# One transformer program on one core: work moved across the edges between its stages

## The reference

```python
def second_block(x, p, norm_g, ...):
    for i in range(DEPTH_2):                      # 2 layers
        g = norm_g[i]
        x = x + FFN_RESIDUAL * rmsnorm_2(swiglu(rmsnorm_2(x, g[0]), ffn_w_in[i, 0], ffn_w_out[i, 0]), g[1])
        h = rmsnorm_2(x, g[2])
        ...                                       # m: diff_attention (i = 0) or s5_glu (i = 1)
        x = x + rmsnorm_2(m, g[3])
        x = x + FFN_RESIDUAL * rmsnorm_2(swiglu(rmsnorm_2(x, g[4]), ffn_w_in[i, 1], ffn_w_out[i, 1]), g[5])
        gate = jax.nn.sigmoid(rmsnorm_2(x, g[6]) @ ple_w_gate[i])
        x = x + rmsnorm_2(gate * (p[i] @ ple_w_proj[i]), g[7])
    return x

def swiglu(h, w_in, w_out):                       # D_FF = 2816
    gu = h @ w_in
    return (jax.nn.silu(gu[..., :D_FF]) * gu[..., D_FF:]) @ w_out
```

## Time and profile before

| | us |
|---|---|
| median of 3 runs | 2223.03 (2222.31 to 2223.61) |
| the profiled execution, its own time | 2225.54 |
| its span, first to last instruction | 2223.8 |
| PE busy | 1993.2 (90%) |
| DVE busy | 1387.0 (62%) |
| ACT busy | 1079.7 (49%) |
| the chain that ended last | PE 65%, DVE 24%, ACT 7%, issue 3%, DMA 1% |
| mean granted TensorE clock | 0.933 |
| a feed-forward unit's transfer, issue to landing (median) | 6.3 |

### The profile page before, as it was taken

The page is one execution under the profiler, slowest core; times in us unless marked ns, Lnnn a source line. Parts: engine busy times, 40 slices in busy tenths (PEclk is TensorE's granted clock), DMA queues, the critical chain, the costliest instruction groups (busy, mean ns, idle before and its releaser), DMA issues.

```text
span 2223.8 us, 29527 instructions
## 1 busy us (share of the span) xinstructions
PE 1993.2 (90%) x11984; PEld 1737.5 (78%) x11984; DVE 1387.0 (62%) x1905; ACT 1079.7 (49%) x1563; POOL 0.2 (0%) x4
## 2 busy tenths in 40 slices
PE   7996899999999978998998899878997599889987
PEld 5885666666666658997887899768997477789976
DVE  4635899999999965564334555435564995255542
ACT  3333788888888864443234434334443221343431
POOL 0000000000000000000000000000000000000000
PEclk9997999999999999998999999999999576999998
DMA  6325888989989864542343454234542000445420
GB/s 243 112 73 199 311 333 330 342 328 341 338 338 336 335 239 154 188 165 73 124 135 149 146 195 167 105 113 156 186 166 91 38 1 23 177 146 195 167 76 19
DMA packets 45661, 408.71 MB, mean 184 GB/s; under 512 B 4800, under 2 KB 10432, under 8 KB 11344
## 3 DMA queue, kind: packets, MB, share of 16 engines
q1 hardware_dynamic: 40688, 398.86, 48.8%
q10 hardware_dynamic: 4832, 7.90, 1.1%
HBM read 405.66 MB, written 1.08 MB: 183 GB/s over the span
## 4 chain that ended last, share of the span: by engine, by line
PE 65%; DVE 24%; ACT 7%; issue 3%; DMA 1%; ACTq 0%; DVEq 0%; SPq 0%
PE wk L1474 23%; DVE ws_moe L1007 12%; PE acc L1455 11%; PE wk L353 7%; ACT ws_moe L1000 3%; PE wk L913 3%; PE wk L1730 3%; PE wk L359 2%; DVE sq L1074 2%; PE wk L959 2%; PE wk L311 2%; DVE rstd L283 2%; PE acc L705 1%; ACT hT L321 1%; PE acc L1759 1%
## 5 line engine op out<-in xcount | busy, mean ns | idle before, releaser
L1007 DVE TENSOR_TENSOR ws_moe<-ring,ws_moe 128x1024 fp32r<-128x1024 f32 x384 | 452.0, 1216 | 41.9 <-ACT ws_moe L1000 41.0
L1000 ACT ACTIVATE ws_moe<-ring 128x1024 fp32r<-128x1024 f32 x384 | 392.0, 1051 | 83.3 <-PE wk L913 72.3
L1474 PE MATMUL wk<-hx,gu_ffn 128*128 128x256 f32 x2112 | 269.0, 288 | 26.6 <-DVE gu_ffn L1404 26.6
L1474 PEld LDWEIGHTS wk<-hx,gu_ffn 128*128 128x128 f32 x2112 | 264.7, 198 | 27.3 <-issue 27.3
L1474 PE MATMUL wk<-hx,gu 128*128 128x256 f32 x2112 | 277.3, 290 | 4.5 <-DVE hx L1491 4.5
L1474 PEld LDWEIGHTS wk<-hx,gu 128*128 128x128 f32 x2112 | 266.1, 195 | 9.1 <-DVE hx L1491 6.7
L959 PE MATMUL wk<-ws_moe,xp_moe 128*128 128x512 f32 x1024 | 271.7, 408 | 1.5 <-issue 1.5
L1455 PE MATMUL acc<-hh_ffn,dn_ffn 128*128 128x256 f32 x2112 | 267.1, 283 | 0.0
L1455 PEld LDWEIGHTS acc<-hh_ffn,dn_ffn 128*128 128x128 f32 x2112 | 259.5, 192 | 0.0
L1434 ACT ACTIVATE hT<-hT 128x256 f32<-128x256 f32 x88 | 36.9, 419 | 392.3 <-DVE hT L1506 392.3
L959 PEld LDWEIGHTS wk<-ws_moe,xp_moe 128*128 128x128 f32 x1024 | 189.6, 190 | 45.1 <-issue 2.4
(11 more groups left out here) (331 smaller groups left out, 2497.3 us busy)
## 6 DMA issues: line engine op xcount, KB each, us to landing
ring<-in_u_moe SPq DMA_DIRECT2D x129, 1536.0 KB, 8.3
ring<-in_u_ffn SPq DMA_DIRECT2D x88, 1536.0 KB, 6.3
ring<-in_u_qkv SPq DMA_DIRECT2D x12, 1024.0 KB, 4.9
ring<-in_u_ple SPq DMA_DIRECT2D x8, 1280.0 KB, 5.4
ring<-in_u_in SPq DMA_DIRECT2D x9, 1024.0 KB, 4.9
ring<-in_u_glu SPq DMA_DIRECT2D x8, 1024.0 KB, 5.0
ring<-in_u_out SPq DMA_DIRECT2D x4, 1024.0 KB, 4.8
ring<-in_u_o SPq DMA_DIRECT2D x4, 1024.0 KB, 5.0
```

The source lines that it names most:

```text
L1000: e.activation(WS[:, n % NWS, 0, :], piece(x), ACT.Copy).then_inc(s.m_hi, 1)
L1007: e.tensor_tensor(WS[:, n % NWS, 1, :], piece(x), WS[:, n % NWS, 0, :].bitcast(F32), SUB).then_inc(s.m_lo, 1)
L1474: m = e.matmul(b[:, a * T:(a + 1) * T], gu_of(c, f)[:, x, a * 1024 + k * 128:a * 1024 + (k + 1) * 128], HX[:, y, k, :], start=k == 0 and a ...
```

## The change

Six things are done:

- In a feed-forward part, the split of unit 1's gate and up weights and of unit 0's down weights stands ahead of the root on ScalarE and ahead of the reciprocal on VectorE. An activation of one column (`tiny`) with Silu stands behind the root.
- A stage's last additions (`add_act`): an activation of one column with Sqrt stands ahead of the copies, and the root stands behind the sixth copy instead of the eighth.
- A feed-forward part's last down products signal after every second tile (`f_end`), and each pair of squares waits for its own.
- The experts' last products signal after every second tile (`m_last`), and VectorE adds in four pairs. ScalarE no longer waits for the fence before unit 0's split, and reads x in part 0 pair by pair. What is still in use at the end of the experts was moved to a second scratch tensor (`scrb`) behind the others, so that unit 0's split may be written early.
- In an embedding all four projections stand ahead of the sums.
- `pT` is fetched in the feed-forward part before, behind its second unit, into a place that this part does not use.

```diff
@@ add_act
+            e.activation(tiny[:, :], cs("eps"), ACT.Sqrt)
             for k in range(8):
                 m = e.activation(hT[:, k, :], src[:, k, :], ACT.Copy, scale=g[:, k:k + 1])
                 if k % 2:
                     m.then_inc(s.gk, 1)
-            root(e, name)
+                if k == 5:
+                    root(e, name)
@@ moe_pe
             for d in range(8):
-                combine_pe(e, NP - 1, d)
+                m = combine_pe(e, NP - 1, d)
+                if d in (1, 3, 5):
+                    m.then_inc(s.m_last, 1)
@@ moe_dve
-            e.wait_ge(s.m_comb, NP)
-            e.tensor_tensor(xT[:, :, :], xT[:, :, :], acc3, ADD).then_inc(s.acc_free, 1)
+            for j in range(4):
+                if j < 3:
+                    e.wait_ge(s.m_last, j + 1)
+                else:
+                    e.wait_ge(s.m_comb, NP)
+                e.tensor_tensor(xT[:, 2 * j:2 * j + 2, :], xT[:, 2 * j:2 * j + 2, :], acc3[:, 2 * j:2 * j + 2, :], ADD).then_inc(s.x_new, 1)
@@ ffn_act
             if c == 0:
-                enter(e, fence_of["ffn", 0])
+                used(e, NH - 1, 3)
                 ffn_early_act(e, 0)
...
             enter(e, fence_of["ffn", c])
+            ffn_split_hi(e, c, 1, False)
+            ffn_split_hi(e, c, 0, True)
+            root(e, ("ffn", c))
+            e.activation(tiny[:, :], cs("zero"), ACT.Silu)
             for f in range(NF):
                 n = c * NF + f
-                if f == 0:
-                    root(e, ("ffn", c))
-                    ffn_split_hi(e, c, 0, True)
-                if f + 1 < NF:
+                if 0 < f < NF - 1:
                     ffn_split_hi(e, c, f + 1, False)
+                if f == 2 and c % 2:
+                    e.dma_start(ple_tiles[c // 2][0], A["pT"][c // 2].rearrange("(k p) t -> p k t", p=128)).then_inc(s.ld_p, 16)
...
-            add_act(e, ("ffn_out", c), acc3, g_out, lambda j: acc_out(e, "ffn", c))
+            add_act(e, ("ffn_out", c), acc3, g_out, lambda j: e.wait_ge(s.f_end, 4 * c + j + 1))
@@ ffn_pe, down
-                m.then_inc(s.f_dn if f < NF - 1 else s.acc_full, 1)
+                    if f == NF - 1 and d % 2:
+                        m.then_inc(s.f_end, 1)
+                if f < NF - 1:
+                    m.then_inc(s.f_dn, 1)
@@ ffn_dve
             enter(e, fence_of["ffn", c])
+            ffn_split_lo(e, c, 1, False)
             ffn_split_lo(e, c, 0, True)
             for f in range(NF):
...
                 if f == 0:
                     row, = inverse(e, ("ffn", c))
-                if f + 1 < NF:
+                elif f + 1 < NF:
                     ffn_split_lo(e, c, f + 1, False)
@@ ple_pe
-            sums_pe(e, ("ple", i))
             e.wait_ge(s.ld_p, 16 * (i + 1))
             acc_in(e, ("ple", i))
             for c in range(4):
                 arrived(e, ("ple", i, c))
...
+            sums_pe(e, ("ple", i))
+            for c in range(4):
+                feature_major(e, K("g", i, c), by_k(tile(("ple", i, c))[:, 0:2048]), hT,
                               new=(lambda t: h_tile(e, ("ple", i), t)) if c == 0 else None)
```

More of the change, by code:

```diff
@@ L108 @@
     "logits gex gexd e2 e2d M flag late h2 sel m_hi m_lo m_used m_gl m_fold m_sil m_act m_tr m_mh m_mhl "
-    "m_yl m_y m_gat m_xh m_xl m_gt m_G m_comb m_shift "
-    "f_gh f_gl f_dh f_dl f_xh f_xl f_xs f_g f_s f_p f_hh f_hl f_dn f_as "
+    "m_last m_yl m_y m_gat m_xh m_xl m_gt m_G m_comb m_shift "
+    "f_gh f_gl f_dh f_dl f_xh f_xl f_xs f_g f_s f_p f_hh f_hl f_dn f_end "
     "ple_y "
@@ L148, in program @@
         flag = sb("flag", [1, 1], I32)
+        tiny = sb("tiny", [128, 1])
         acc = ctx.enter_context(nc.psum_tensor("acc", [128, 4, 512], F32))
@@ L193, in program @@
         fulls = Order()
-        fulls.then(("att", 0, 0), ("att", 0, 1), ("att", 1, 0), ("att", 1, 1), "gla", *[("ffn", c) for c in range(4)])
+        fulls.then(("att", 0, 0), ("att", 0, 1), ("att", 1, 0), ("att", 1, 1), "gla")
         x_at = Order()
-        x_at.then("mix", ("ffn", 0), "o", ("ffn", 1), ("ple", 0), ("ffn", 2), "ssm", ("ffn", 3), ("ple", 1))
+        x_at.then("mix", "moe", ("ffn", 0), "o", ("ffn", 1), ("ple", 0), ("ffn", 2), "ssm", ("ffn", 3), ("ple", 1))
         sq_at = Order()
@@ L201, in program @@
         g_at.then(("ffn_out", 0), "o_out", ("ffn_out", 1), ("ple_out", 0), ("ffn_out", 2), "z", ("ffn_out", 3), ("ple_out", 1))
-        gave = {"mix": (s.acc_free, 6), "moe": (s.x_new, 4), ("ffn", 0): (s.acc_free, 7)}
+        gave = {"mix": (s.acc_free, 6), "moe": (s.x_new, 4), ("ffn", 0): (s.x_new, 8)}
         for n, name in enumerate(("o", ("ffn", 1), ("ple", 0), ("ffn", 2), "ssm", ("ffn", 3), ("ple", 1))):
@@ L796, in mixer_dve @@
                 e.tensor_tensor(xT[:, 2 * c:2 * c + 2, :], xT[:, 2 * c:2 * c + 2, :], acc3[:, 2 * c:2 * c + 2, :], ADD).then_inc(s.x_new, 1)
-        S2SIZE = 4900
-        scr2, WS, Xp, MH, gtail, shift = area(
+        S2SIZE = 3880
+        scr2, WS, Xp, MH, gtail, shift, scr2b = area(
             "_moe", ("scr", [128, S2SIZE], F32), ("ws", [128, NWS, 2, 1024], F32R), ("xp", [128, 2, 2, 8, 128], F32R),
-            ("mh", [128, 2, 2, 128], F32R), ("gt", [128, 512], F32R), ("sh", [128, 64], F32R))
+            ("mh", [128, 2, 2, 128], F32R), ("gt", [128, 512], F32R), ("sh", [128, 64], F32R), ("scrb", [128, 1024], F32))
         S2 = Scr(scr2, S2SIZE)
+        S2b = Scr(scr2b, 1024)
         L = S2.get(2, 36)
@@ L815, in program @@
         SG = [S2.get(2, 128) for _ in range(2)]
-        GT_ = [S2.get(T) for _ in range(2)]
+        GT_ = [S2b.get(T) for _ in range(2)]
         ysm = [sq[:, 4 * x:4 * x + 4, :].rearrange("p a t -> p (a t)") for x in range(2)]
-        msil = [S2.get(T) for _ in range(2)]
+        msil = [S2b.get(T) for _ in range(2)]
         gm, goh, gex, gsum = R[:, :, 0:1], R[:, :, 1:5], R[:, :, 5:9], R[:, :, 9:10]
@@ L883, in combine_pe @@
                 m.then_inc(s.m_comb, 1)
+            return m
         def share_pe(e, u):
@@ L1361, in program @@
                     for c in range(4)]
+        FFN_AREA = 4096 + 6144 + 1024
         def gu_of(c, f):
@@ L1379, in ffn_g @@
             return sm("norm_g", a, a + 8), sm("norm_g", a + 8, a + 16)
-        before_ffn = {1: "o", 2: ("ple", 0), 3: "ssm"}
+        before_ffn = {0: "moe", 1: "o", 2: ("ple", 0), 3: "ssm"}
         def ffn_split_hi(e, c, f, dn):
@@ L1419, in ffn_act @@
             for k in range(8):
-                if c and k % 2 == 0:
+                if k % 2 == 0:
                     x_pair(e, before_ffn[c], k // 2)
@@ L1522, in ple_area @@
         def ple_area(i):
-            scr, = area(f"_ple{i}", ("scr", [128, 2560], F32))
-            S = Scr(scr, 2560)
-            return S.get(2, T), S.get(8, T)
+            sg, _, pTt = area(f"_ple{i}", ("sg", [128, 8, T], F32), ("pad", [128, FFN_AREA - 8 * T], F32), ("pt", [128, 2, T], F32))
+            return pTt[:, :, :], sg[:, :, :]
         ple_tiles = [ple_area(i) for i in range(2)]
@@ L1542, in ple_act @@
             enter(e, fence_of["ple", i])
-            e.dma_start(pTt, A["pT"][i].rearrange("(k p) t -> p k t", p=128)).then_inc(s.ld_p, 16)
             for c in range(4):
@@ L1559, in ple_pe @@
                 arrived(e, ("ple", i, c))
-                w = tile(("ple", i, c))
-                wp = by_k(w[:, 2048:2560], 2)
+                wp = by_k(tile(("ple", i, c))[:, 2048:2560], 2)
                 for k in range(2):
@@ L1565, in ple_pe @@
                                  stop=k == 1, skip_group_check=True)
-                feature_major(e, K("g", i, c), by_k(w[:, 0:2048]), hT,
+            sums_pe(e, ("ple", i))
+            for c in range(4):
+                feature_major(e, K("g", i, c), by_k(tile(("ple", i, c))[:, 0:2048]), hT,
                               new=(lambda t: h_tile(e, ("ple", i), t)) if c == 0 else None)
```

## The result

The changed kernel took 2154.37 us (median of 4 runs, 2153.18 to 2156.17) against 2223.32 for the kernel before: a ratio of 0.9691, 95% interval 0.9675 to 0.9708. The forecast was 2161 us in a range of 2152 to 2174. A second measurement, with new runs of the kernel before beside it, gave 2155.06 us, ratio 0.9696 (0.968 to 0.9712). The profiled execution took 2155.44 us around a span of 2153.6, so 70.1 us of span are gone where the steps of the prediction sum to 62.0.

The account below looks back on a forecast made before the run. TensorE, busy 90% of the span, was taken as the bound, its waits at stage edges as the loss. Gains of 37.5 + 3.9 + 1.6 + 7.7 + 11.3 = 62.0 us from the 2223.0 median gave 2161 us, range 2152 to 2174.

Parts of the forecast that it names:

- Unit 1 ahead of the root: Four feed-forward parts: unit 1 follows unit 0 at once; 37.5 us together, including 3.7 us from the mixture's end.
- Mixture's end in pairs: Experts' end into part 0: adding pairs as they come starts TensorE sooner; 3.7 us gained, bounds 3.0 to 4.7.
- A stage's last additions: Stage ends: earlier squares and root; 1.95 us per part end, 0.55 at the embeddings' and state-space ends.
- Embedding 1: Last embedding: projections ahead of the sums let gate products end sooner; 11.3 us with the preceding part's end.
- Embedding 0: First embedding: projections ahead of the sums let gate products end sooner; 7.7 us with the preceding part's end.
- Rival (a): Embeddings: clock falls in the new waits, costing 2.9 us for one, 6 for both: 2167 us; chance 0.13.
- (b): Feed-forward parts: the wait moves to unit 2 and later units, losing 17 us: 2178 us; chance 0.07.
- (c): Feed-forward parts: unit 1's weights land late and hold the multiplies; 2245 us if 26 us late; chance 0.02.
- (d): Parts' edit fails through fence or table load; only embedding and ends stay, 24 us: 2199 us; chance 0.04.

Follow-up runs that it names:

- warm_edges: Changed kernel plus products of constants in TensorE's waits at the stage edges; 2145.71 us, ratio 0.9665 to the kernel before.
- part0: Kernel before with only the mixture's end and part 0 edited (pairs, unit 0 split without the fence, unit 1 ahead of the root, scratch moved); 2204.05 us, ratio 0.991.
- split123: Kernel before with only unit 1 split ahead of the root in parts 1 to 3; 2211.35 us, ratio 0.9945.
- the delay run: split123 plus four one-column activations (some 0.8 us) between the state-space stage's sums and its root; 2202.6 us.
- warm_both: Changed kernel with products of constants in edge and routing waits, plus two ahead of each of 16 state-space driving steps; 2141.26 us, ratio 0.9632.

## Why the prediction came out as it did

- **Unit 1 ahead of the root** held. The wait is gone in all four parts, unit 1 took 5.92 us in part 0, and parts 1 to 3 alone gave 24.05 us for 24.8. Unit 2 didn't wait in part 0, where I had left 1.4 us. The table load, which I took to stay on the root's path, moved beside unit 0's products; it accounts for 1.28 us of that.
- **Mixture's end in pairs** was mis-sized: 3.7 us forecast, 2.2 measured (PE starts 9.96 us behind the last expert products' start, 12.17 before). The step that failed is the 1.5 us for branch and drain, read off ScalarE; VectorE stood for 2.98. My lower bound of 3.0, with 2.2 us for it, did not hold that. With part 0's own gain, which was larger than forecast, the two errors nearly cancel, by luck: 13.0 us for 12.7.
- **A stage's last additions**: 2.13 us for 1.95 in the parts, 0.69 for 0.55 at the other ends. Small and on the same side. Ahead of the two embeddings the 2.13 us stand in the part's interval and are lost again in the next one, since the small products wait for the eighth copy. The prediction's 7.7 and 11.3 were worked out by that queue, and the second came out as 11.2; my later division of them, 1.95 for the end and the rest for the embedding, was wrong.
- **Embedding 1** held: 9.8 us for 9.9 without part 3's end. **Embedding 0** gave 3.1 for 6.3. Rival (a) named the reason: a clock that falls in the new waits. It came true in one embedding of two and cost 3.1 us, by warm_edges, where it was priced at 2.9 a piece. Against the second profile of the kernel before the same embedding gained 6.5 us, so the 3.1 leans on the profile that it is taken from; the low clock in the changed kernel doesn't, it came in both of its profiles.
- **The unedited stages** are what the sum left out. I priced the clock only where an edit stood. The attention gave 2.5 us, the routing 2.7 (gathers 3.84 us instead of 6.12, transposes 3.25 instead of 3.65), the expert products behind it 0.4, and the state-space stage 5.9 beyond its end. The single edits and the repeats show that this last term changes without any edit in the stage, from 207 us in part0 to 231 in split123, and the routing's 2.7 were gone again in warm_edges. So the surplus of 8 us over the forecast is no result of a step that I forecast, and in split123 the rest of the program took 13 us instead. The range held because its lower end allowed restarts in the parts to vanish, not because it knew of this.
- **Rivals (b), (c), (d)** did not come: unit 2 waits 0.2 us or less, the weights were there, and each part gave its term.

What stays open: why the changed kernel repeats within 0.1 us in every stage where the kernel before does not. Two profiles each don't tell whether it is a property of the kernel. Open too is what decides where the clock falls in an unedited stage; the delay run was to show it and doesn't.

## What to carry to other kernels

Sum an edit's effect over the stretch that it touches, by queues, and judge it there: in the four kernels with one edit each the steps held within 1.4 us root to root, in the embeddings by luck, while the times were off by up to 13. Edits that meet at one edge need one sum over both: what the one saves there the other may already wait for. Look at the clock in the stages that you don't touch, and repeat the profile, before you credit or blame an edit. Where TensorE waits, at the stages' edges and in the routing, filling the waits with products of constants gave 18 us in the medians here, more than three of the four edits did in their own intervals.

## What the runs showed of the hardware

- TensorE's granted clock stayed at 0.50 over 47.4 and 61.8 us in which the engine was busy without a pause, with products of 32 rows or columns. Two full-size products ahead of each step raised it to 0.89 over 47.4 us at the same place (warm_both).
- One stage with the same instructions took from 206.6 us at a mean granted clock of 0.79 to 231.2 us at 0.65, and two executions of one program differed by 5.7 us in it (216.8 and 211.1).
- A table load waited for the sums of the root behind it when that root stood directly behind the fence: its 1.28 us lay on the root's path before, and beside other work once a split stood there. After an activation the load itself followed with 0.02 us between.
- Across the flag's branch and drain at the mixture's end VectorE stood idle for 2.98 us and ScalarE for 2.29, with no wait that the trace names.
